# Second layer's down projection in two column halves, 19 of its 44 steps by seven block products, left-hand sums kept in memory

## The chip, the cores and the metric

The kernel runs on one core of a Trainium2 chip. The core's engines are TensorE (PE in the profile; its weight loads are PEld), VectorE (DVE), ScalarE (ACT), GpSimd (POOL) and SyncE (SP, which here only issues DMAs). The metric is device time in microseconds (us) of one execution; lower is better.

## The reference

Two decoder layers over 256 tokens, model width 2048, everything float32. Attention and the state-space mixer are not touched by this change, so only the end of a layer is shown.

```python
for l in range(DEPTH):                     # DEPTH = 2
    h = rms_norm(x, attn_norm_w[l])
    ...                                    # attention and SSD mixer, joined in mixed
    x = x + mixed
    h = rms_norm(x, ffn_norm_w[l])
    ff = (silu(h @ w_gate[l]) * (h @ w_up[l])) @ w_down[l]   # (256, 5632) @ (5632, 2048)
    x = x + ff
```

## The kernel before

**Three products for one.** Each float32 operand is split in a high part (a rounding to the type fp32r) and a low part (the rest), and each block product is three matmuls: high by high, low by high, high by low. The activations after the gate are kept so, as `f_hi` and `f_lo` (44 tiles of 128 rows by 256 tokens). Weights come from memory in pairs: a pair is 256 rows of a weight by 512 columns, 512 KB, in one of four slots of the ring `raw` (RING = 4). SyncE loads it once VectorE has split the pair four before it (`lo_split`); ScalarE writes the high part (L912; it waits until TensorE has used the pair four before, `pair_used`); VectorE subtracts to get the low part (L1169). Both do this LEAD = 3 pairs ahead of TensorE's place. So each engine walks through the same numbered pairs p = 0, 1, ..., and the rest of its work is hung on certain p in its own loop. All of it is written out by hand with semaphores; an engine does its list in order.

**The stages of a layer.** 72 pairs of the input projection, 32 of the output projection (from P_OUT), 176 of gate and up (from P_FF: 11 chunks of 512 columns, 8 pairs of gate and 8 of up each), 88 of down (from P_DOWN: four column blocks n of 512, 22 pairs each). Where the weights are the stationary operand ("turned", L744) a pair is 24 matmuls of 256 columns. In layer 1's down the activations are stationary and the weights move: a pair is 12 matmuls of 512 columns (L547; the last pair is L559, `last_products`, which does one token half after the other).

**Where the weights' high and low parts lie.** `w_hi`, `w_hi_s` and `w_hi_e` name the same ring of slots at three small offsets (0, 64 and 224 bytes on); `w_lo` likewise. Turned pairs use `_s`, and the pairs p in FURTHER_ON use `_e`. All of these are in slot 3.

**Layer 1's down in detail.** `products` adds token halves t = 0 and 1 of block n into two PSUM banks; the pairs of banks 0, 1 and 2, 3 alternate over the n. After the block, VectorE scales the two banks by the norm factor `rs` and adds them to `xr` (`add_down`, L1433). `xr` holds x turned by 128x128 tiles after the mixer, so it is turned back first: 8 transposes (`turn_back`, L581) after pair 2 of each block, and two copies on ScalarE (`back_out`, L962). SyncE stores block n while block n+1 runs, and the last block in two token halves (`store_last`, L362).

**The gate.** `form_ff` (L1451) writes silu(gate) times up for a chunk into `stage[:, 1]`; ScalarE and VectorE split it into `f_hi` (L1056) and `f_lo` (L1457).

## Time and profile before

| what | us |
|---|---|
| three timed runs: median, lowest, highest | 2111.05, 2110.71, 2111.59 |
| the profiled execution: its own time, its span | 2112.05, 2110.0 |
| TensorE, VectorE, ScalarE, GpSimd busy | 2101.6, 1269.3, 983.6, 134.3 |
| layer 1's gate and up end, down begins | 1863.5 |
| last matmul begins | 2106.3 |

The span is first to last instruction; the profiled execution's own time is 2.05 us more, and the median of the timed runs is 1.0 us under that time. A matmul's duration in the profile is from entering to leaving the array, so that matmuls overlap: their rate is read from how long a run of so many takes, not from the mean duration.

### The profile page before, as it was taken

How to read it: one execution, taken by the hardware profiler on the slowest of the kernel's cores; microseconds unless marked ns; L12 is line 12 of the kernel's file. 1: busy time of each engine (PE TensorE's matmuls, PEld its weight loads, DVE VectorE, ACT ScalarE, POOL GpSimd, SP SyncE). 2: the span in 40 equal slices, each digit the busy share in tenths (PEclk: the TensorE clock that was granted, in tenths of full speed). 3: DMA queues.
4: the chain of work that ended last, by engine and by line, in shares of the span. 5: the costliest groups of instructions: out<-in, count | busy, mean ns of one | idle time of the engine just before them, and what ended most of it. 6: DMA issues, size and time to landing. Idle time of an engine off the chain costs nothing.

```text
span 2110.0 us, 38413 instructions
## 1 busy us (share of the span) xinstructions
PE 2101.6 (100%) x16853; PEld 1998.7 (95%) x16853; DVE 1269.3 (60%) x1455; ACT 983.6 (47%) x1215; POOL 134.3 (6%) x158
## 2 busy tenths in 40 slices
PE   9999999999999999999999999999999999999999
PEld 8987899999999999999999878999999999988887
DVE  6887866555555555555578878665555555544443
ACT  5555754444444444443445556544444444443332
POOL 1034200000000000000000432000000000000000
PEclk9999999999999999999999999999999999999999
DMA  7675466666666666666666644666666666666664
GB/s 224 181 214 151 128 199 194 197 192 194 195 192 197 192 194 195 192 192 198 192 175 190 199 146 148 193 190 195 194 193 197 192 195 194 192 191 201 198 206 131
DMA packets 204518, 397.24 MB, mean 188 GB/s; under 512 B 12400, under 2 KB 12800, under 8 KB 204352
## 3 DMA queue, kind: packets, MB, share of 16 engines
q1 hardware_dynamic: 202752, 390.24, 62.6%
q0 software_dynamic: 1568, 4.56, 0.9%
q8 instruction: 132, 2.16, 0.4%
q14 instruction: 34, 0.28, 0.0%
q10 hardware_dynamic: 32, 0.01, 0.0%
HBM read 392.62 MB, written 2.13 MB: 187 GB/s over the span
## 4 chain that ended last, share of the span: by engine, by line
PE 98%; DMA 1%; ACT 1%; DVE 0%; issue 0%; SPq 0%; ACTq 0%
PE ps L744 72%; PE ps L547 22%; PE ps L581 1%; PE ps L723 1%; DMA raw<-in_w_in_dram 0%; PE ps L701 0%; PE ps L700 0%; PE ps L676 0%; DMA xr<-in_x_dram 0%; PE ps L661 0%; PE ps L623 0%; PE ps L652 0%; ACT w_hi_s L912 0%; PE ps L559 0%; SPq L326 0%
## 5 line engine op out<-in xcount | busy, mean ns | idle before, releaser
L1169 DVE TENSOR_TENSOR w_lo_s<-raw,w_hi_s 128x1024 fp32r<-128x1024 f32 x553 | 681.7, 1233 | 606.4 <-ACT w_hi_s L912 605.3
L912 ACT CAST w_hi_s<-raw 128x1024 fp32r<-128x1024 f32 x553 | 580.5, 1050 | 783.0 <-PE ps L744 767.7
L744 PE MATMUL ps<-h_hi,w_hi_s 128*128 128x256 f32 x3224 | 892.4, 277 | 1.5 <-DVE h_lo L1178 0.9
L744 PE MATMUL ps<-h_hi,w_lo_s 128*128 128x256 f32 x3224 | 890.8, 276 | 0.0
L744 PE MATMUL ps<-h_lo,w_hi_s 128*128 128x256 f32 x3224 | 890.7, 276 | 0.0
L744 PEld LDWEIGHTS ps<-h_hi,w_hi_s 128*128 128x128 f32 x3224 | 605.5, 188 | 2.1 <-DVE h_lo L1178 1.1
L744 PEld LDWEIGHTS ps<-h_lo,w_hi_s 128*128 128x128 f32 x3224 | 605.5, 188 | 0.0
L744 PEld LDWEIGHTS ps<-h_hi,w_lo_s 128*128 128x128 f32 x3224 | 605.4, 188 | 0.0
L744 PE MATMUL ps<-f_hi,w_hi_s 128*128 128x256 f32 x1192 | 330.3, 277 | 0.0
L744 PE MATMUL ps<-f_hi,w_lo_s 128*128 128x256 f32 x1192 | 329.5, 276 | 0.0
L744 PE MATMUL ps<-f_lo,w_hi_s 128*128 128x256 f32 x1192 | 329.5, 276 | 0.0
L1169 DVE TENSOR_TENSOR w_lo<-raw,w_hi 128x1024 fp32r<-128x1024 f32 x168 | 211.0, 1263 | 146.5 <-ACT w_hi L912 146.3
L912 ACT CAST w_hi<-raw 128x1024 fp32r<-128x1024 f32 x168 | 175.3, 1050 | 177.0 <-PE ps L547 166.4
L744 PEld LDWEIGHTS ps<-f_hi,w_hi_s 128*128 128x128 f32 x1192 | 223.8, 188 | 0.8 <-issue 0.7
L744 PEld LDWEIGHTS ps<-f_hi,w_lo_s 128*128 128x128 f32 x1192 | 224.0, 188 | 0.0
L744 PEld LDWEIGHTS ps<-f_lo,w_hi_s 128*128 128x128 f32 x1192 | 223.8, 188 | 0.1
L547 PE MATMUL ps<-w_hi,f_hi 128*128 128x512 f32 x348 | 107.5, 390 | 0.0
L547 PE MATMUL ps<-w_hi,f_lo 128*128 128x512 f32 x348 | 107.2, 389 | 0.0
L547 PE MATMUL ps<-w_lo,f_hi 128*128 128x512 f32 x348 | 107.1, 389 | 0.0
L547 PE MATMUL ps<-w_hi,h_hi 128*128 128x512 f32 x320 | 102.6, 402 | 0.0
L547 PE MATMUL ps<-w_hi,h_lo 128*128 128x512 f32 x320 | 98.9, 390 | 0.0
L547 PE MATMUL ps<-w_lo,h_hi 128*128 128x512 f32 x320 | 98.8, 390 | 0.0
(224 smaller groups left out, 1535.0 us busy)
## 6 DMA issues: line engine op xcount, KB each, us to landing
raw<-in_w_gate_dram SPq DMA_DIRECT2D x176, 512.0 KB, 4.4
raw<-in_w_up_dram SPq DMA_DIRECT2D x176, 512.0 KB, 4.4
raw<-in_w_down_dram SPq DMA_DIRECT2D x176, 512.0 KB, 4.2
raw<-in_w_in_dram SPq DMA_DIRECT2D x144, 512.0 KB, 3.7
raw<-in_w_out_dram SPq DMA_DIRECT2D x64, 512.0 KB, 4.2
cum_all<-cum_kept POOLq DMA_DIRECT2D x8, 512.0 KB, 4.8
xr<-in_x_dram SPq DMA_DIRECT2D x4, 512.0 KB, 9.0
out_dram<-xr SPq DMA_DIRECT2D x3, 512.0 KB, 5.9
```

Of the source, the lines that this page charges most:

```text
L547: done = nc.tensor.matmul(ps[:, bank + t, :], lhs[:, rows + k, t * P:(t + 1) * P], w[:, slot, k, :], start=(first and k == 0 and w is w_hi ...
L581: done = nc.tensor.transpose(ps[0:src.shape[1], bank + at // N, at % N:at % N + src.shape[0]], src, ident[0:src.shape[0], 0:src.shape[0]])
L723: last = nc.tensor.matmul(ps[half * HEAD:(half + 1) * HEAD, 5, keys * P:TOK], vtok[:, keys, j, :], pT[:, half, keys * TOK:TOK + keys * P], ...
L744: done = nc.tensor.matmul(ps[:, bank + m // 2, m % 2 * TOK:(m % 2 + 1) * TOK], w[:, slot, k, m * P:(m + 1) * P], h[:, rows + k, :], start= ...
L912: nc.scalar.copy(split_buffers(pair)[0][:, slot, :, :], raw[:, slot, :, :]).then_inc(hi_split, 1)
L1169: v_.tensor_tensor(lo[:, slot, :, :], raw[:, slot, :, :], hi[:, slot, :, :].bitcast(F32), ALU.subtract).then_inc(lo_split, 1)
```

## The change

**Steps instead of blocks.** Layer 1's down goes in two column halves of 1024. A step is 256 rows of `w_down` by such a half: two pairs, e = 0 and 1 (22 steps in a half, 44 in all). SyncE's load order follows. With the activations of a step as 2x2 blocks A (128 rows k by 128 tokens t) and the weights as 2x2 blocks B (k by 512 columns e), an ordinary step has eight block products, 24 matmuls (`eight_products`, L649). In steps 3, 5, ..., 19 of the first half and 1, 3, ..., 19 of the second (9 + 10 = 19) it has seven, 21 matmuls (`seven_products`, L664 to L666), by the Winograd form of Strassen's method. The four partial results of that form that more than one output shares are added up over all such steps in four PSUM banks (`sum_banks`), the other products go to the four ordinary output banks (`four_banks`); so eight banks are in use, and the two halves swap the groups. Which sums are formed:

- of the activations, four blocks of 128x128 for an odd step: GpSimd forms them as `s_raw` from `stage[:, 1]` right after `form_ff`, ScalarE and VectorE split them, GpSimd stores both parts to memory (`s_kept`, 512 KB a chunk, 10 chunks), and in the down stage loads them back into a ring of two (`load_left`, 19 loads of 512 KB);
- of the weights, four blocks of 128x512: VectorE forms them as `t_raw` (`right_sums`, one operation of 1024 columns and two of 512), ScalarE and VectorE split them (`t_hi`, `t_lo`, which lie in `h_hi` and `h_lo`; two operations of 1024 on each). Of the second pair only half has to be split itself.

**After a half** VectorE adds the shared sums: `sums_out` parts 0 to 3 (an addition and a `grow`, which scales and adds to `xr`) at its places P_DOWN + 40 to 43 of the half, then `four_out` twice (two `grow` each). ScalarE first copies one bank (`keep_first`). TensorE waits for part 3 (`sums_added`) before the second half's step 0.

**Moved.** The 32 transposes of `turn_back` now stand in layer 1's gate and up, 16 after pair P_FF + 10 and 16 after P_FF + 14; `back_out` with them, at ScalarE's places P_FF + 11 and 15. P_FF + 15 joins FURTHER_ON, in both layers. The stores of blocks 0 and 1 go out in the second half, block 2's behind the last load.

```diff
+    STEPS = {0: range(3, 20, 2), 1: range(1, 20, 2)}
+    FORMS = FCH - 1
...
+    def seven_before(half, q):
+        return half * len(STEPS[0]) + len([s for s in STEPS[half] if s < q])
...
+    def four_banks(half):
+        return [[4, 6], [5, 7]] if half == 0 else [[0, 2], [1, 3]]
+    def sum_banks(half):
+        return (0, 1, 2, 3) if half == 0 else (4, 5, 6, 7)
...
-        FURTHER_ON = (7, 15, 19, 27, P_OUT + 7, P_FF + 7, P_FF + 11, P_DOWN + 3)
+        FURTHER_ON = (7, 15, 19, 27, P_OUT + 7, P_FF + 7, P_FF + 11, P_FF + 15, P_DOWN + 3)
...
+                    if layer == DEPTH - 1:
+                        half, q, e = down_step(layer * PAIRS + p)
+                        n = 2 * half + e
...
-                    if layer == DEPTH - 1 and p >= P_DOWN + DOWN and (p - P_DOWN) % DOWN == 8:
-                        store((p - P_DOWN) // DOWN - 1)
+                    if layer == DEPTH - 1 and p in (P_DOWN + 2 * DOWN + 10, P_DOWN + 2 * DOWN + 14):
+                        store((p - P_DOWN - 2 * DOWN - 10) // 4)
+            store(2)
...
+                v = stage[:, 1, 1, :]
+                a11, a21, a12, a22 = (v[:, i * P:(i + 1) * P] for i in range(4))
+                own.done(pool.tensor_tensor(s_raw[:, 0, :], a21, a22, ALU.add))
+                own.done(pool.tensor_tensor(s_raw[:, 1, :], s_raw[:, 0, :], a11, ALU.subtract))
+                pool.tensor_tensor(s_raw[:, 2, :], a11, a21, ALU.subtract)
+                pool.tensor_tensor(s_raw[:, 3, :], a12, s_raw[:, 1, :], ALU.subtract).then_inc(s_formed, 1)
...
+                pool.dma_start(s_kept[c, :, 0, :, :], s_hi).then_inc(s_stored, 16)
+                pool.dma_start(s_kept[c, :, 1, :, :], s_raw.bitcast(F32R)).then_inc(s_stored, 16)
...
+                i = seven_before(half, q)
+                if i >= 2:
+                    pool.wait_ge(s_used, i - 1)
+                pool.dma_start(s_ring[:, i % 2], s_kept[q // 2]).then_inc(s_landed[i % 2], 16)
...
+            def seven_products(pair, half, q):
...
+                i, slot = seven_before(half, q), pair % RING
+                first, last = q == STEPS[half][0], q == STEPS[half][-1]
+                (b11, b12), (b21, _) = four_banks(half)
+                b1, b5, b7, b6 = sum_banks(half)
+                s = s_ring[:, i % 2]
+                def product(bank, left_hi, left_lo, right_hi, right_lo, opens=False, closes=False):
+                    nc.tensor.matmul(ps[:, bank, :], left_hi, right_hi, start=opens, stop=False)
+                    nc.tensor.matmul(ps[:, bank, :], left_lo, right_hi, start=False, stop=False)
+                    return nc.tensor.matmul(ps[:, bank, :], left_hi, right_lo, start=False, stop=closes)
...
+                pe.wait_ge(lo_split, pair + (1 + RING))
+                product(b1, *left(0, 0), w_hi[:, slot, 0, :], w_lo[:, slot, 0, :], first, last)
+                product(b11, *left(1, 0), w_hi[:, slot, 1, :], w_lo[:, slot, 1, :]).then_inc(pair_used, 1)
+                pe.wait_ge(lo_split, pair + (2 + RING))
+                pe.wait_ge(s_landed[i % 2], 16 * (i // 2 + 1))
+                product(b12, *mixed(3), w_hi[:, slot + 1, 1, :], w_lo[:, slot + 1, 1, :]).then_inc(pair_used, 1)
+                pe.wait_ge(t_split, 2 * i + 1)
+                product(b5, *mixed(0), *summed(0, 0), first, last)
+                product(b7, *mixed(2), *summed(0, 1), first, last).then_inc(t_used, 1)
+                pe.wait_ge(t_split, 2 * i + 2)
+                product(b6, *mixed(1), *summed(1, 0), first, last).then_inc(s_used, 1)
+                product(b21, *left(1, 1), *summed(1, 1)).then_inc(t_used, 1)
...
+                        if layer == DEPTH - 1 and c == 0 and q in (2, 6):
+                            if q == 2:
+                                pe.wait_ge(rsb_ready, layer * 2 + 2)
+                            else:
+                                pe.wait_ge(back_ready, 2)
+                            for n in range(q // 2 - 1, q // 2 + 1):
+                                turn_back(n)
...
+                            if half and q == 0:
+                                pe.wait_ge(sums_added, 1)
+                            if half and q == STEPS[1][0]:
+                                pe.wait_ge(down_added, layer * DCH + 2)
+                            if seven(pair):
+                                seven_products(pair, half, q)
+                            else:
+                                eight_products(pair, half, q, 0)
...
-                nc.scalar.copy(split_buffers(pair)[0][:, slot, :, :], raw[:, slot, :, :]).then_inc(hi_split, 1)
+                if not seven(pair) or down_step(pair)[2] == 0:
+                    nc.scalar.copy(split_buffers(pair)[0][:, slot, :, :], raw[:, slot, :, :]).then_inc(hi_split, 1)
+                    return
+                nc.scalar.copy(w_hi[:, slot, 1, :], raw[:, slot, 1, :]).then_inc(hi_split, 1)
+                i = seven_before(*down_step(pair)[:2])
+                for a in range(2):
+                    act.wait_ge(t_formed, 2 * i + a + 1)
+                    if i:
+                        act.wait_ge(t_used, 2 * i + a - 1)
+                    nc.scalar.copy(t_hi[:, a], t_raw[:, a]).then_inc(t_hi_ready, 1)
...
+            def keep_first(half):
+                act.wait_ge(t_used, 2 * seven_before(half, DOWN))
+                nc.scalar.copy(stage[:, 0, 0, :], ps[:, sum_banks(half)[0], :]).then_inc(first_kept, 1)
...
+                v_.tensor_tensor(lo[:, slot, 1, :], raw[:, slot, 1, :], hi[:, slot, 1, :].bitcast(F32),
...
+                for a in range(2):
+                    dve.wait_ge(t_hi_ready, 2 * i + a + 1)
+                    v_.tensor_tensor(t_lo[:, a], t_raw[:, a], t_hi[:, a].bitcast(F32), ALU.subtract).then_inc(t_split, 1)
...
+            def right_sums(pair):
+                slot, i = pair % RING, seven_before(*down_step(pair)[:2])
+                if i == 0:
+                    dve.wait_ge(pair_used, (DEPTH - 1) * PAIRS + P_DOWN + RING)
+                else:
+                    dve.wait_ge(t_split, 2 * i)
+                for j in range(2):
+                    dve.wait_ge(raw_landed[slot + j], 16 * (pair // RING + 1))
+                v_.tensor_tensor(t_raw[:, 0], raw[:, slot + 1, :, :], raw[:, slot:slot + 2, 0, :], ALU.subtract) \
+                    .then_inc(t_formed, 1)
+                dve.wait_ge(t_formed, 2 * i + 1)
+                own.done(v_.tensor_tensor(t_raw[:, 1, 0, :], raw[:, slot + 1, 1, :], t_raw[:, 0, 0, :], ALU.subtract))
+                v_.tensor_tensor(t_raw[:, 1, 1, :], raw[:, slot, 1, :], t_raw[:, 1, 0, :], ALU.subtract) \
+                    .then_inc(t_formed, 1)
...
+                u1, u2, u4, u5 = stage[:, 0, 0, :], stage[:, 0, 1, :], stage[:, 1, 0, :], stage[:, 1, 1, :]
+                if part == 0:
+                    dve.wait_ge(first_kept, half + 1)
+                    own.done(v_.tensor_tensor(u2, b6, u1, ALU.add))
+                    grow(rows(0, 0), 0, b1)
+                if part == 1:
+                    own.done(v_.tensor_tensor(u4, b5, u2, ALU.add))
+                    grow(rows(0, 1), 0, u4)
+                if part == 2:
+                    own.done(v_.tensor_tensor(u5, b7, u4, ALU.add))
+                    grow(rows(1, 1), 1, u5)
+                if part == 3:
+                    own.done(v_.tensor_tensor(u2, b7, u2, ALU.add))
+                    grow(rows(1, 0), 1, u2).then_inc(sums_added, 1)
+                    dve.wait_ge(sums_added, half + 1)
...
+            def four_out(half, e):
...
+                    last = v_.scalar_tensor_tensor(v, ps[:, four_banks(half)[t][e], :], rs[:, t:t + 1], v,
+                                                   ALU.mult, ALU.add)
...
-                    if base + p + LEAD < ALL:
-                        split_lo(base + p + LEAD)
+                    ahead_pair = base + p + LEAD
+                    if ahead_pair < ALL:
+                        if seven(ahead_pair) and down_step(ahead_pair)[2] == 0:
+                            right_sums(ahead_pair)
+                        split_lo(ahead_pair)
...
+                        half, q, e = down_step(base + p)
+                        if q >= DOWN - 2:
+                            sums_out(half, 2 * (q - DOWN + 2) + e)
+                        if q == DOWN - 1 and e:
+                            four_out(half, 0)
+                            four_out(half, 1)
```

TensorE in layer 1's down, before, around the transposes of a block (`f_hi`, `f_lo` are the activations):

```order
L547 MATMUL ps<-w_hi,f_hi 128x512 x2
L547 MATMUL ps<-w_hi,f_lo 128x512 x2
L547 MATMUL ps<-w_lo,f_hi 128x512 x2
L581 MATMUL ps<-ident,xr 128x128 x8
L547 MATMUL ps<-w_hi,f_hi 128x512 x2
```

and now, in a step of seven, three of its block products (`h_lo` is here the ring of loaded sums as left operand and `t_lo` as right one, `h_hi` is `t_hi`):

```order
L664 MATMUL ps<-w_hi,f_hi 128x512
L665 MATMUL ps<-w_hi,f_lo 128x512
L666 MATMUL ps<-w_lo,f_hi 128x512
L664 MATMUL ps<-w_hi,h_lo 128x512
L665 MATMUL ps<-w_hi,h_lo 128x512
L666 MATMUL ps<-w_lo,h_lo 128x512
L664 MATMUL ps<-h_hi,h_lo 128x512
L665 MATMUL ps<-h_hi,h_lo 128x512
L666 MATMUL ps<-h_lo 128x512
```

The pairs' x2 (both token halves by one weight block) became triples that each go to one bank, and the transposes have left the stage.

TensorE in layer 1's first chunk of the up projection, before, where pair P_FF + 10 ends and the pair P_FF + 11, in `_e`, begins:

```order
L744 MATMUL ps<-h_hi,w_hi_s 128x256
L744 MATMUL ps<-h_lo,w_hi_s 128x256
L744 MATMUL ps<-h_hi,w_lo_s 128x256
L744 MATMUL ps<-h_hi,w_hi_e 128x256
L744 MATMUL ps<-h_lo,w_hi_e 128x256
```

and now:

```order
L871 MATMUL ps<-h_hi,w_hi_s 128x256
L871 MATMUL ps<-h_lo,w_hi_s 128x256
L871 MATMUL ps<-h_hi,w_lo_s 128x256
L708 MATMUL ps<-ident,xr 128x128 x16
L871 MATMUL ps<-h_hi,w_hi_e 128x256
L871 MATMUL ps<-h_lo,w_hi_e 128x256
L871 MATMUL ps<-h_hi,w_lo_e 128x256
```

Sixteen transposes came between the two; the same stands after P_FF + 14, whose next pair is now in `_e` too.

VectorE in layer 1's down, before, from the first block's end on (`add_down` is L1433):

```order
L1169 TENSOR_TENSOR w_lo<-raw,w_hi 128x1024 x20
L1433 SCALAR_TENSOR_TENSOR xr<-ps,rs,xr 128x512 x2
L1169 TENSOR_TENSOR w_lo<-raw,w_hi 128x1024 x22
L1433 SCALAR_TENSOR_TENSOR xr<-ps,rs,xr 128x512 x2
L1169 TENSOR_TENSOR w_lo<-raw,w_hi 128x1024 x22
```

and now, at the end of the first half, from part 1 of `sums_out` on (L1391, L1394, L1397 are additions of parts 1, 2, 3; L1383 is `grow`; L1363 to L1367 are `right_sums`; L1414 is `four_out`):

```order
L1391 TENSOR_TENSOR stage<-ps,stage 128x512
L1383 SCALAR_TENSOR_TENSOR xr<-stage,rs,xr 128x512
L1344 TENSOR_TENSOR w_lo<-raw,w_hi 128x1024
L1394 TENSOR_TENSOR stage<-ps,stage 128x512
L1383 SCALAR_TENSOR_TENSOR xr<-stage,rs,xr 128x512
L1363 TENSOR_TENSOR t_raw<-raw 128x1024
L1366 TENSOR_TENSOR t_raw<-raw,t_raw 128x512
L1367 TENSOR_TENSOR t_raw<-raw,t_raw 128x512
L1344 TENSOR_TENSOR w_lo<-raw,w_hi 128x1024
L1397 TENSOR_TENSOR stage<-ps,stage 128x512
L1383 SCALAR_TENSOR_TENSOR xr<-stage,rs,xr 128x512
L1414 SCALAR_TENSOR_TENSOR xr<-ps,rs,xr 128x512 x4
```

The right-hand sums of the second half's step 1 and the split of its first pair stand ahead of part 3, for which TensorE waits.

## Rows read from the trace of the kernel before

**Rows 1.** The page, chain that ended last: shares of the span by engine.
```profile
PE 98%; DMA 1%; ACT 1%; DVE 0%; issue 0%; SPq 0%; ACTq 0%
```

**Rows 2.** Chain that ended last, 1800 to 2110: start us, us, what.
```profile
1799.89 63.81 PE ps L744 x563
...
1871.89 0.88 PE ps L581 x8
1872.77 59.85 PE ps L547 x264
...
2103.97 2.73 PE ps L559 x12
...
2106.73 0.75 DVE xr L1433
```

**Rows 3.** Busy by window: PE, PEld, DVE, ACT, POOL; clock, DMA share, GB/s.
```profile
1950.00:2000.00 50.00, 50.00 (x226) 41.46 (x225) 23.38 (x20) 19.97 (x21) 0.00 (x0) 1.00 0.66 196
```

**Rows 4.** Groups, 1880 to 2110: busy us, mean ns of one, idle before.
```profile
L1169 DVE TENSOR_TENSOR w_lo<-raw,w_hi 128x1024 fp32r<-128x1024 f32 x80 | 98.0, 1225 | 117.2 <-ACT w_hi L912 117.2
L912 ACT CAST w_hi<-raw 128x1024 fp32r<-128x1024 f32 x79 | 82.9, 1049 | 124.3 <-PE ps L547 124.3
...
L1433 DVE SCALAR_TENSOR_TENSOR xr<-ps,rs,xr 128x512 f32<-128x512 f32 x8 | 5.7, 748 | 8.9 <-PE ps L559 7.8 <-PE ps L547 1.1
L962 ACT COPY xr<-ps 128x512 f32<-128x512 f32 x6 | 3.2, 590 | 7.5 <-PE ps L581 7.5
```

**Rows 5.** Timeline of VectorE, 1863 to 1867.5: start, duration, instruction.
```profile
1863.74 1.23 DVE L1451 TENSOR_TENSOR stage<-ps,stage 128x1024 f32<-128x1024 f32 x1 [0.36 <-PE ps L744]
1864.88 1.23 DVE L1169 TENSOR_TENSOR w_lo<-raw,w_hi 128x1024 fp32r<-128x1024 f32 x1
```

**Rows 6.** Timeline, all engines, 1990 to 2012: a pair's start and its split.
```profile
2005.00 0.62 PE L547 MATMUL ps<-w_hi,f_hi 128*128 128x512 f32 x2
...
2005.25 1.05 ACT L912 CAST w_hi<-raw 128x1024 fp32r<-128x1024 f32 x1 [1.67 <-PE ps L547]
...
2006.33 1.23 DVE L1169 TENSOR_TENSOR w_lo<-raw,w_hi 128x1024 fp32r<-128x1024 f32 x1 [1.50 <-ACT w_hi L912]
```

**Rows 7.** Landing of `w_down` loads, all 176.
```profile
DMA to landing us min/median/max: 3.5/4.2/5.9
```

**Rows 8.** `cum_all`'s loads by GpSimd: issue ns, and landing.
```profile
L480 POOL DMA_DIRECT2D cum_all<-cum_kept x8: 530/590/635, 112.5 to 1191.0; - x8
...
DMA to landing us min/median/max: 4.1/4.8/6.1
```

**Rows 9.** DMA rate in 40 slices of 2080 to 2110; landing of its stores.
```profile
GB/s 96 229 320 87 117 322 219 71 145 358 145 112 248 303 46 0 0 0 0 0 0 0 0 0 0 0 0 0 0 0 0 0 0 0 0 0 344 63 292 0
...
out_dram<-xr SPq DMA_DIRECT2D x2, 256.0 KB, 2.1
```

**Rows 10.** The page's DMA issues: the stores of 512 KB.
```profile
out_dram<-xr SPq DMA_DIRECT2D x3, 512.0 KB, 5.9
```

**Rows 11.** Chain, 1250 to 1500, layer 1's P_FF + 4 and on.
```profile
1397.50 0.34 PE ps L605 x4
1397.84 11.30 PE ps L744 x96
...
1409.35 90.66 PE ps L744 x799
```

**Rows 12.** Chain, 1060 to 1120, layer 1's first pairs.
```profile
1075.70 8.47 PE ps L744 x72
...
1086.40 11.31 PE ps L744 x96
```

**Rows 13.** Tile `w_hi_e`, 1070 to 1090: where its matmuls stand.
```profile
L744 PE MATMUL ps<-h_hi,w_hi_e x8: 277/279/281, 1078.5 to 1080.9; 128*128 128x256 f32 x8
```

**Rows 14.** Waits of TensorE over the span: total us, times, longest.
```profile
PE ps L744 <- DVE h_lo L1178: 0.9, 1, 0.9
```

**Rows 15.** Tile `dist` on GpSimd: an addition of 128x128.
```profile
L422 POOL TENSOR_TENSOR dist<-dist,ahead x1: 454/454/454, 4.2 to 4.2; 128x128 f32<-128x128 f32 x1
```

More of the change, by code:

```diff
@@ L92, in weights_stationary, with down_step, seven @@
         return p < 4 * PPG or P_OUT <= p < P_DOWN or p >= P_DOWN and layer < DEPTH - 1
+    def down_step(pair):
+        layer, p = pair // PAIRS, pair % PAIRS
+        if layer < DEPTH - 1 or p < P_DOWN:
+            return None
+        half, rest = divmod(p - P_DOWN, 2 * DOWN)
+        return half, rest // 2, rest % 2
+    def seven(pair):
+        step = down_step(pair)
+        return step is not None and step[1] in STEPS[step[0]]
+    def seven_before(half, q):
[4 more added lines that the diff above has]
+        return (0, 1, 2, 3) if half == 0 else (4, 5, 6, 7)
     def bank_of(layer, idx):
@@ L154, in split_buffers @@
             return (w_hi_e, w_lo_e) if pair % PAIRS in FURTHER_ON else (w_hi_s, w_lo_s)
+        at_h = 83456
         xr = sb("xr", [P, T, D], F32, 128)
@@ L551, in products, with last_products @@
                 done.then_inc(pair_used, 1)
-            def last_products(slot, pair, rows, bank):
+            def last_products(slot, pair, rows, banks):
                 pe.wait_ge(lo_split, pair + (1 + RING))
@@ L558, in last_products, with eight_products @@
                         for lhs, w in ((f_hi, w_hi), (f_lo, w_hi), (f_hi, w_lo)):
-                            done = nc.tensor.matmul(ps[:, bank + t, :], lhs[:, rows + k, t * P:(t + 1) * P],
+                            done = nc.tensor.matmul(ps[:, banks[t], :], lhs[:, rows + k, t * P:(t + 1) * P],
                                                     w[:, slot, k, :], start=False, stop=(k == 1 and w is w_lo))
                     done.then_inc((half_done, pair_used)[t], 1)
+            def eight_products(pair, half, q, e):
+                slot, last = pair % RING, q == DOWN - 1
+                pe.wait_ge(lo_split, pair + (1 + RING))
+                for k in range(2):
+                    for lhs, w in ((f_hi, w_hi), (f_lo, w_hi), (f_hi, w_lo)):
+                        for t in range(T):
+                            done = nc.tensor.matmul(ps[:, four_banks(half)[t][e], :],
+                                                    lhs[:, 2 * q + k, t * P:(t + 1) * P], w[:, slot, k, :],
+                                                    start=(q == 0 and k == 0 and w is w_hi and lhs is f_hi),
+                                                    stop=(last and k == 1 and w is w_lo))
+                done.then_inc(pair_used, 1)
@@ new lines, in left_lo, with sums_out, rows, grow @@
+            def left_lo(c):
+                dve.wait_ge(s_hi_ready, c + 1)
+                v_.tensor_tensor(s_raw.bitcast(F32R), s_raw, s_hi.bitcast(F32), ALU.subtract).then_inc(s_split, 1)
+            def sums_out(half, part):
+                b1, b5, b7, b6 = (ps[:, b, :] for b in sum_banks(half))
+                def rows(t, e):
+                    n = 2 * half + e
+                    return xr[:, t, n * N:(n + 1) * N]
+                def grow(v, t, by):
+                    return v_.scalar_tensor_tensor(v, by, rs[:, t:t + 1], v, ALU.mult, ALU.add)
+                u1, u2, u4, u5 = stage[:, 0, 0, :], stage[:, 0, 1, :], stage[:, 1, 0, :], stage[:, 1, 1, :]
[13 more added lines that the diff above has]
+                    dve.wait_ge(sums_added, half + 1)
@@ new lines, in four_out @@
+            def four_out(half, e):
+                n = 2 * half + e
+                final = n == DCH - 1
+                if not final:
+                    dve.wait_ge(pair_used, (DEPTH - 1) * PAIRS + P_DOWN + 2 * (half + 1) * DOWN - 1 + e + RING)
+                for t in range(T):
+                    v = xr[:, t, n * N:(n + 1) * N]
+                    if final and t == 0:
+                        dve.wait_ge(half_done, 1)
+                    elif final:
+                        last.then_inc(down_added, 1)
+                        dve.wait_ge(pair_used, ALL + RING)
+                    last = v_.scalar_tensor_tensor(v, ps[:, four_banks(half)[t][e], :], rs[:, t:t + 1], v,
+                                                   ALU.mult, ALU.add)
+                last.then_inc(down_added, 1)
```

112 lines of the change are left out of this document (78 added, 34 removed).

## Prediction, made before the run

> **What bounds the kernel.** I read first the chain that ended last. It is TensorE for 98% of the span, with nothing in it that another engine holds up [rows 1]: so a matmul taken away is worth its whole interval, and a matmul that has to wait costs the whole wait. Then the rates. In layer 1's down 264 matmuls of 512 columns take 59.85 us, 226.7 ns each; the last twelve, which go six in a row to one bank, take 2.73 us, 227.5 ns each, so neither the order of the banks nor the wait at each pair shows [rows 2]. A pair of 12 is 2.72 us. In the turned stage before it 563 matmuls of 256 columns take 63.81 us, 113.3 ns each [rows 2]. Last, what stands beside: in 50 us of down VectorE is busy 23.4 and ScalarE 20.0, the granted clock is 1.00 (the 2.4 GHz level) and the DMA engines are busy 0.66 of the time at 196 GB/s [rows 3].
>
> **What goes.** A step of seven has 21 matmuls for 24. 19 steps x 3 x 226.7 ns = 12.92 us [rows 2]. The operands keep their size, and each is 512-byte aligned as before, so I take the same rate for the triples into one bank, on the evidence of the last twelve; the far end is a rate of 227.5 for all 399 matmuls of these steps, 0.3 us, and below nothing I see no reason for a gain.
>
> **What moves.** Four groups of eight transposes, 0.88 us each [rows 2], leave down and cost the same in gate and up: nought. Their copies are 8 x 0.59 us on ScalarE [rows 4]. They go in two lots of 2.4 us, while a pair is split once in 2.72 us with 1.05 of work and three pairs of lead: covered.
>
> **Does the feed keep up?** From the issue of one step of seven to the next, with one of eight between, TensorE now has 45 matmuls, 10.20 us. Let the first begin at 0: its first pair is used at 1.36, its second at 2.04, `t_hi`'s first half at 3.40, all at 4.76; the step of eight uses its pairs at 7.48 and 10.20. Latencies: ScalarE starts 0.25 us after a pair's end and takes 1.05, VectorE follows 0.03 later [rows 6]. VectorE's 1024 columns last 1.23 us, but the next operation starts after 1.14 [rows 5]; 512 columns no row shows behind another: half of 1.14 is 0.57, and 0.75 is one alone out of PSUM [rows 4]. I take 0.6 in the steps and 0.75 for the sums after a half, which read PSUM. Where one waits for the one before I add 0.1. VectorE: split of the last pair before, done at 2.5; right-hand sums of the next step, 1.14 + 0.7 + 0.7, done at 5.05 (with 0.75 for 0.6, three times a round, 0.45 more of its 10.20); split of its first pair 6.2, half of its second 6.8, `t_lo` 7.95 and 9.1; the next pair's split 10.25; then it idles 1.3 us until ScalarE has the high part of the pair that comes free at 10.20, at 11.5, and is done at 12.7, that is 2.5 of the next round. The circle closes: VectorE has 8.9 us of work in 10.20. TensorE wants the first pair at 10.20 (it was there at 6.2), `t_lo` at 12.24 and 13.6 (there at 7.95 and 9.1): at least 4.0 us of slack. So nothing is lost in the steps themselves. If that cover went, a round would last as long as VectorE's work.
>
> **Loads.** The sums need `w_down`'s second pair, whose load is issued when the half split of the second pair before is done, at -3.4, and is wanted at 2.5: 5.9 us. Loads land in 3.5 to 5.9, median 4.2 [rows 7]; beside GpSimd's loads of the same size those take 4.1 to 6.1 [rows 8]. Traffic rises to five loads of 512 KB in 10.20 us, 257 GB/s, DMA busy 0.66 x 257/196 = 0.87; single slices reach 358 GB/s [rows 9]. Here three loads are issued within 2 us (-5.2, -4.0, -3.4), 1.5 MB, 4.4 us at that rate, so I expect 5 to 5.5 for the last. A landing 0.3 late a round would eat 5 us of idle time and slack over a half: hardly visible. Cost taken: 0, ends 0 and 3.
>
> **The middle (a new wait).** Before, one block's sums were added while the next block used two other banks. Now all eight are in use, and the second half's step 0 needs the banks of the shared sums. Let T be the end of the last step of seven of the first half; four pairs follow, so TensorE is ready at T + 10.88. VectorE has split pair 43 of the stage at T + 0.25. `keep_first` runs T + 0.25 to 0.85. Part 0 (two of 0.75 at most [rows 4]) ends at 2.4. Pair 44 is free to be overwritten at 2.72, its high part there at 4.0, low part at 5.2; part 1 ends at 6.7. Pair 45: 6.75 and 7.95; part 2 ends at 9.4. Now, ahead of part 3, come the right-hand sums of pair 46 (2.55) and its split (1.15): 13.1. Part 3 ends at 14.65. TensorE starts at about 14.85: **it waits 4.0 us**. Queued behind the waiting matmul is all of TensorE's work; behind VectorE's part 3 are four `grow` and the split of pair 47, which end at 17.8 and 18.4 and are wanted by step 1 at 20.3 and 21.7: no second wait. Ends: 2.5, if the operations of 512 columns overlap as those of 1024 do, and 5.5, if each of the eight dependences costs 0.3 more than I gave it.
>
> The chip may take that wait amiss. The granted clock is 1.00 in every window, and after the start TensorE never idles longer than 0.9 us [rows 14], so no row tells what 4 us of idleness do. If TensorE came back at the 1.2 GHz level, half the clock could at worst double the 226.7 ns of the next step's 24 matmuls: +5.4 us. I take 0 and keep the other end for the range. On this the Trainium skill ("TensorE: Matmul & The Clock Gate", section "Part 1: The HAM clock gate") says that an idle TensorE drops to 1.2 GHz, the low level, and has to be busy for a while to get the high one back: a rule that speaks against the change, and no run here yet shows it.
>
> **The end.** `sums_out` of the second half lies under the last four pairs (no split stands between, part 3 ends at T' + 6.5), and the last `grow` of 0.75 after the last matmul is as before [rows 2]. But block 2's store of 512 KB, before under the last block, is now issued about 1.8 us before the last 256 KB: 1 MB in 2 us. The last landed in 2.1; 512 KB ones took 5.9 under load [rows 9, 10]. At 344 GB/s [rows 9] 1 MB takes 3.0 us, so the last lands 0.6 later; ends 0 and 2.
>
> **Gate and up, layer 1.** GpSimd's four additions are about 0.45 each [rows 15], over a whole chunk of 43 us; ScalarE's and VectorE's extra 512 columns fit in their idle time; a store of 512 KB a chunk adds 12 GB/s. Nought. The further `_e` pair in each layer costs at most the slow rate of rival A, 0.106 us: 0.2.
>
> **Sum**: -12.9 + 4.0 + 0.6 + 0.2 + 0 = -8.1 us. The profiled execution took 2112.05, so 2103.9; the median of the runs is 1.0 less, **2103**.
>
> **Rivals.**
>
> *A, slower: the turned stage stays at its slow rate.* The stage has two rates. After a foreign matmul at P_FF + 4 the next 96 go at 11.30 us, 117.7 ns, and with the pair after the `_e` pair the rate is back at 113.4 [rows 11]. In layer 1's first pairs an `_e` pair [rows 13] did not do it: 72 matmuls with it in their middle took 117.6 ns each and the 96 behind 117.8 [rows 12]. The change puts 32 transposes in front of the FF's fast stretch, with an `_e` pair directly behind each lot, a placing that no row shows. If the slow rate survives P_FF + 15, 160 pairs follow at 24 x 4.4 ns = 0.106 us more: +16.9, 2120. It decides from 77 slow pairs on (8.1 / 0.106). For it: one failure in the trace; against: the later `_e` pairs all restored the rate, and slow stretches there were short.
>
> *B: loads or VectorE bind.* If the last load of a bunch takes L, a round is at least 4.3 + L. At L = 6.3 that is 10.6; 17 rounds lose 6.8 less the slack of 4 in each half, mostly hidden, but the middle's wait grows by what VectorE is behind, up to 4: 2107. At L = 7, 11.3 a round, 19 less 8 of slack: 2114; from L = 7.1 it is slower by what can be told. For it: 0.87 of the DMA time and bunches; against: 6.1 is the longest seen beside GpSimd's loads. The Trainium skill ("Trainium Kernel Development and Optimization", section "Key Constraints") states that DMAs issued by SP and by GpSimd share the same 16 engines and interleave, which agrees with the longer landings [rows 8] and speaks for B: a second queue would bring no second path.
>
> *C: the middle costs nothing*, or little, since VectorE is faster than I count: 2099 to 2100.
>
> *D: the clock falls after the wait*, for all or part of the next step: 2105 to 2108. For and against: above, at the middle.
>
> *E: the products don't run at 226.7*, since three left operands come from freshly loaded memory and the right one from another place; at 236 ns (4% more) the 399 matmuls give 3.7 us back: 2106.7. Nothing in the trace speaks for it.
>
> **Numbers.** Forecast 0.62 (2101 to 2105.5), A 0.10, B 0.10 (a third of it slower or no gain), C 0.07, D 0.07, E 0.04. What a measurement of this kernel can tell from no change is about 0.2%, 4.2 us: faster is under 2106.8, slower over 2115.3. Faster: forecast, C, most of D, half of E and of B: 0.80; same 0.09 (the rest of B, D and E); slower 0.11 (A and the worst of B). The range leaves out A and the worst of B: 2099 to 2110.
>
> **What would show it.** Right: down lasts 243.2 - 3.5 - 12.9 + 4.0 = 231 us; triples at 226.7 ns; one wait of TensorE of about 4 us on VectorE between the halves, and no other over 0.3; VectorE busy near 88% in down; gate and up at 113.3 from P_FF + 16 on. Wrong: many small waits of TensorE on `t_lo` (B), 117.7 ns through gate and up (A), a granted clock under 1.00 after the middle (D). A time over 2110 would refute the sum, one under 2099 the wait in the middle.

## The result, and the profile after

| kernel | median us (lowest to highest) | ratio to before, 95% interval |
|---|---|---|
| before | 2110.88 (2110.52 to 2111.59) | 1 |
| changed | 2121.57 (2121.04 to 2122.30) | 1.0050 (1.0033 to 1.0068) |

The change made the kernel slower by 10.7 us; 2103 was forecast, 2110 was the upper end. Of all executions used below one, of 7500 us, of `after_sums_first_b`, was disturbed: it is among the five of that median and not in the ratio beside it. The profiled execution of the changed kernel took 2121.89 us, its span is 2120.2, 10.2 more than before. That splits by stage:

| stretch | before | changed | difference |
|---|---|---|---|
| start to the matmuls of `x_total` in layer 1 (after P_FF + 4) | 1397.50 | 1396.76 | -0.7 |
| from there to the first matmul of layer 1's down | 466.0 | 487.0 | +21.0 |
| down, first to last matmul | 242.8 | 232.6 | -10.1 |
| last matmul to the end | 3.7 | 3.75 | +0.05 |

So down gained nearly what was promised, and gate and up lost twice that. The chain that ended last, changed kernel, 1380 to 2125 (start, us, what), to be held against [rows 11]:

```profile
1396.76 0.34 PE ps L732 x4
1397.10 11.30 PE ps L871 x96
...
1414.09 1.75 PE ps L708 x16
1415.83 11.29 PE ps L871 x96
1427.12 1.75 PE ps L708 x16
1428.87 455.08 PE ps L871 x3864
```

After the first lot of transposes 96 matmuls take 11.29 us, 117.6 ns each, and after the second lot all 3864 of the rest take 117.8 ns. Before, the same stretch ran at 113.3: in 350 us of gate and up 3091 matmuls began before and 2974 now. The two rows, before and changed, in that order (columns as in [rows 3]):

```profile
1500.00:1850.00 350.00, 350.00 (x3091) 350.00 (x3090) 185.38 (x153) 151.75 (x145) 0.00 (x0) 1.00 0.67 194
```

```profile
1500.00:1850.00 350.00, 350.00 (x2974) 350.00 (x2974) 183.97 (x156) 150.72 (x148) 29.42 (x46) 1.00 0.67 197
```

TensorE's row reads "busy 350.00 of 350.00" in both, and the granted clock is 1.00 in both. Only the count tells that the engine is 4% slower. Down itself, from the same chain: an ordinary step is 5.44 us as before, and the steps of seven follow at the same interval.

```profile
1905.05 5.44 PE ps L649 x24
1910.72 0.23 PE ps L665
1910.95 0.23 PE ps L666
...
1915.25 5.44 PE ps L649 x24
...
2001.04 8.32 PE ps L649 x24
...
2114.09 2.73 PE ps L638 x12
2116.84 0.75 DVE xr L1414
```

From 1905.05 to 1915.25 is 10.20 us for the 45 matmuls of two steps, 226.7 ns each. One ordinary step, at 2001.04, took 8.32: it is the first of the second half, right behind the wait in the middle. TensorE's waits (total, times, longest), then the windows around it:

```profile
PE ps L649 <- DVE xr L1383: 3.5, 1, 3.5
PE ps L895 <- POOL numbers L455: 2.2, 1, 2.2
```

```profile
1996.00:2001.00 5.00, 1.53 (x7) 0.94 (x5) 4.89 (x6) 2.51 (x3) 0.00 (x0) 0.87 0.35 99
2001.00:2006.00 5.00, 4.96 (x12) 3.89 (x13) 4.97 (x7) 0.00 (x0) 0.00 (x0) 0.50 0.42 120
2006.00:2011.00 5.00, 5.00 (x22) 4.09 (x21) 2.30 (x3) 2.28 (x3) 0.00 (x0) 0.95 0.43 127
```

The granted clock, 1.00 until then, is 0.50 (the 1.2 GHz level) for the 5 us behind the wait, and the matmuls that begin there are 427 ns apart. The next matmul had been due at 1997.37, so the wait cost 3.67 us; the 3.5 of the list is counted from the modelled end of the last one. What VectorE did in the wait (its timeline, 1993 to 2001.5):

```profile
1995.13 0.75 DVE L1383 SCALAR_TENSOR_TENSOR xr<-stage,rs,xr 128x512 f32<-128x512 f32 x1
1995.80 1.22 DVE L1363 TENSOR_TENSOR t_raw<-raw 128x1024 f32<-128x1024 f32 x1
1997.05 0.69 DVE L1366 TENSOR_TENSOR t_raw<-raw,t_raw 128x512 f32<-128x512 f32 x1
1997.78 0.69 DVE L1367 TENSOR_TENSOR t_raw<-raw,t_raw 128x512 f32<-128x512 f32 x1
1998.39 1.22 DVE L1344 TENSOR_TENSOR w_lo<-raw,w_hi 128x1024 fp32r<-128x1024 f32 x1
1999.52 0.68 DVE L1397 TENSOR_TENSOR stage<-ps,stage 128x512 f32<-128x512 f32 x1
2000.24 0.75 DVE L1383 SCALAR_TENSOR_TENSOR xr<-stage,rs,xr 128x512 f32<-128x512 f32 x1
```

The right-hand sums (2.6 us) and a split (1.1 us) stand between part 2 and part 3, as the order of the program has it. Part 3 ends at 2000.99, and TensorE goes on at 2001.04.

The landing of all 176 loads of `w_down`, for [rows 7], and who waited for them (us, times):

```profile
  ACT w_hi L1064: 20.7, 17
  DVE t_raw L1363: 15.5, 15
...
DMA to landing us min/median/max: 3.5/4.4/7.1
```

A load takes up to 7.1 us, VectorE waits for loads 15 times ahead of the right-hand sums, and yet TensorE's list of waits in down has no load and no `w_lo`: the slack covers it. The last three stores (512, 256, 256 KB) land in 2.7, 2.8 and 2.1 us, so the tail is as long as before.

Down accounts for itself: -12.9 (57 matmuls), -3.9 (the transposes left: 3.5, and 0.35 at the four returns from them), +3.7 (the wait), +2.9 (8.32 - 5.44, the low clock) gives -10.2, and -10.1 was measured. What had to be found out is the +21.0: 3.5 are the transposes that moved in, and the 96 and 3864 matmuls behind them, 466.4 us in the chain above, would have taken 448.7 at 113.3 ns: 17.7. Together that is 21.2; the 0.2 too much is rounding and the pair P_FF + 11 in `_e`, which took 2.80 us for 2.72 in the kernel before too.

### The profile page after: what moved, and what is told of

Same layout as the page of the kernel before. It is cut to its first block, busy times and chain, and to the rows that moved or that the text cites. A ratio compares the mean times of both kernels' runs of the same rounds, so it can differ in the third digit from the quotient of the medians.

```text
span 2120.2 us, 38631 instructions
## 1 busy us (share of the span) xinstructions
PE 2107.9 (99%) x16796; PEld 2006.3 (95%) x16796; DVE 1362.8 (64%) x1576; ACT 1020.0 (48%) x1265; POOL 183.3 (9%) x237
## 4 chain that ended last, share of the span: by engine, by line
PE 98%; ACT 1%; DVE 1%; issue 0%; DMA 0%; ACTq 0%
PE ps L871 73%; PE ps L626 10%; PE ps L649 6%; PE ps L666 1%; PE ps L665 1%; PE ps L664 1%; PE ps L708 1%; PE ps L850 1%; PE ps L828 0%; PE ps L827 0%; PE ps L803 0%; DMA xr<-in_x_dram 0%; ACT stage L1112 0%; PE ps L788 0%; DMA raw<-in_w_in_dram 0%
## 5 line engine op out<-in xcount | busy, mean ns | idle before, releaser
L1064 ACT CAST w_hi<-raw 128x1024 fp32r<-128x1024 f32 x149 | 155.4, 1051 | 119.2 <-PE ps L649 47.5
L1344 DVE TENSOR_TENSOR w_lo<-raw,w_hi 128x1024 fp32r<-128x1024 f32 x149 | 186.6, 1264 | 37.5 <-ACT w_hi L1064 36.9
L626 PEld LDWEIGHTS ps<-w_hi,h_hi 128*128 128x128 f32 x320 | 58.4, 188 | 16.1 <-issue 5.3
L626 PEld LDWEIGHTS ps<-w_hi,h_lo 128*128 128x128 f32 x320 | 60.1, 188 | 12.8
```

The costliest lines, as they stand in the source:

```text
L626: done = nc.tensor.matmul(ps[:, bank + t, :], lhs[:, rows + k, t * P:(t + 1) * P], w[:, slot, k, :], start=(first and k == 0 and w is w_hi ...
L1064: nc.scalar.copy(split_buffers(pair)[0][:, slot, :, :], raw[:, slot, :, :]).then_inc(hi_split, 1)
L1344: v_.tensor_tensor(lo[:, slot, :, :], raw[:, slot, :, :], hi[:, slot, :, :].bitcast(F32), ALU.subtract).then_inc(lo_split, 1)
```

## Experiments

Each time beside a ratio is the median of its runs, with the runs of the kernel before on the same chip.

**1. Which part makes gate and up slow?** The change brings three things there: transposes, GpSimd's sums with their stores, and a further `_e` pair. `before_moved_b` is the kernel before with the transposes and their copies moved and with the further `_e` pair, without the sums:

```diff
-        FURTHER_ON = (..., P_FF + 7, P_FF + 11, P_DOWN + 3)
+        FURTHER_ON = (..., P_FF + 7, P_FF + 11, P_FF + 15, P_DOWN + 3)
...
+                        if layer == DEPTH - 1 and c == 0 and q in (2, 6):
...
+                            for n in range(q // 2 - 1, q // 2 + 1):
+                                turn_back(n)
...
-                        if layer == DEPTH - 1 and q == 2:
-                            turn_back(n)
```

> The kernel before with one part of the change alone: the 32 transposes and their copies stand in layer 1's gate and up (16 after pair P_FF + 10, 16 after P_FF + 14) and P_FF + 15 is an _e pair; down is in blocks of eight products as before. Theory 1 (the transposes put the turned stage at its slow rate and the _e pair directly behind does not end it) and theory 2 (so many transposes leave a slow state that no _e pair ends) both say: 160 pairs at 117.8 instead of 113.3 ns, 24 x 4.5 ns x 160 = 17.3 us, so about 2128. Theory 3 (the slow rate comes from the other parts of the change, GpSimd's sums and stores or the longer program): about 2111, gate and up at 113.3.

Measured: 2128.99, ratio 1.0082 (1.0067 to 1.0097), 18 us over before, with nothing of Strassen in it. Its chain and its window of 350 us:

```profile
1416.04 11.29 PE ps L744 x96
1427.33 1.75 PE ps L581 x16
1429.08 71.00 PE ps L744 x603
```

```profile
1500.00:1850.00 350.00, 350.00 (x2974) 350.00 (x2973) 179.17 (x148) 146.68 (x140) 0.00 (x0) 1.00 0.65 187
```

The same 2974 matmuls, with GpSimd idle (0.00) and no more GB/s than before. So it is not the sums, their stores or their memory. That it is not the `_e` pair either, part 4 shows, which takes it out. The copies of `back_out` (2.4 us of ScalarE a lot) always came with the transposes, and no run tells the two apart, though the matmuls stay slow for 455 us after the last copy.

**2. Can an `_e` pair farther behind give the rate back?** `after_e19_b` is the changed kernel with the `_e` pair four pairs later:

```diff
-        FURTHER_ON = (..., P_FF + 11, P_FF + 15, P_DOWN + 3)
+        FURTHER_ON = (..., P_FF + 11, P_FF + 19, P_DOWN + 3)
```

> The changed kernel with P_FF + 19 in FURTHER_ON in place of P_FF + 15: the last lot of transposes (after P_FF + 14) is followed by four ordinary pairs, the last three before the _e pair being those of slots 0, 1, 2. Theory 1: 113.3 ns from P_FF + 20 on, 156 pairs x 0.108 = 16.8 us less than the changed kernel, about 2104.7. Theories 2 and 3: still slow, 2121.6.

Measured: 2104.94, ratio 0.9968 (0.9955 to 0.9981).

```profile
1427.76 1.75 PE ps L708 x16
1429.51 70.57 PE ps L871 x618
```

```profile
1500.00:1850.00 350.00, 350.00 (x3090) 350.00 (x3089) 190.91 (x161) 156.93 (x154) 30.62 (x48) 1.00 0.71 206
```

The matmuls are slow up to P_FF + 19, and fast from P_FF + 20 to the end of the stage. One number in the code is worth 16.6 us. So the loss is the rate of the matmuls and nothing else: the work is the same, transposes included, at the same places.

`after_slot0_b` puts each lot of transposes ahead of two ordinary pairs and these ahead of an `_e` pair:

```diff
-                        if layer == DEPTH - 1 and c == 0 and q in (2, 6):
+                        if layer == DEPTH - 1 and c == 0 and q == 4:
...
+                        if layer == DEPTH - 1 and c == 1 and q == 0:
...
+        FURTHER_ON = (..., P_FF + 11, P_FF + 15, P_FF + 19, P_DOWN + 3)
```

> The changed kernel with the two lots of transposes after pairs P_FF + 12 and P_FF + 16 (slot 0) and _e pairs at P_FF + 15 and P_FF + 19, so two ordinary pairs and then the _e pair follow each lot, as in the places of the kernel before where the rate came back. Theory 1: 113.3 ns from P_FF + 20 on, about 2104.6. Theories 2 and 3: 2121.6.

Measured: 2104.25, ratio 0.9967 (0.9955 to 0.9980). In its chain the 96 matmuls after a lot take 11.20 us, two slow pairs, the `_e` pair and a fast one; then 576 take 65.57, 113.8 each.

**3. How many ordinary pairs does it take?** `after_slot1`: the second lot one pair later, so that one ordinary pair stands between it and the `_e` pair.

```diff
-                        if layer == DEPTH - 1 and c == 1 and q == 0:
+                        if layer == DEPTH - 1 and c == 1 and q == 1:
```

> The changed kernel with the first lot of transposes after P_FF + 12 (slot 0) and the second after P_FF + 17 (slot 1), _e pairs at P_FF + 15 and P_FF + 19: one ordinary pair stands between the second lot and its _e pair. If an _e pair ends the slow rate only with two or more ordinary pairs ahead of it (as all places show where it did), gate and up stay at 117.8 ns from P_FF + 18 on: 156 pairs x 0.108 = 16.8 us over the 2104.25 of the kernel with two, about 2121. If one pair is enough: 2104.

Measured: 2105.18 in one run, which with its window of 3091 matmuls is enough to tell it from 2121. One ordinary pair is enough here. Yet in [rows 12] of the kernel before one ordinary pair stood there too, and the rate did not come back. What tells these two apart stays open.

**4. Is it the `_e` pair at all?** Three kernels without it. `after_no_e15` is the changed kernel, `slot0_v2_no_e` is `slot0_v2` (below), `before_no_e` the kernel before:

```diff
-        FURTHER_ON = (..., P_FF + 7, P_FF + 11, P_FF + 15, P_DOWN + 3)
+        FURTHER_ON = (..., P_FF + 7, P_FF + 11, P_DOWN + 3)
```

```diff
-        FURTHER_ON = (..., P_FF + 7, P_FF + 11, P_FF + 15, P_FF + 19, P_DOWN + 3)
+        FURTHER_ON = (..., P_FF + 7, P_FF + 11, P_DOWN + 3)
```

```diff
-        FURTHER_ON = (..., P_OUT + 7, P_FF + 7, P_FF + 11, P_DOWN + 3)
+        FURTHER_ON = (..., P_OUT + 7, P_DOWN + 3)
```

> The changed kernel without its new _e pair P_FF + 15. If an _e pair directly behind transposes does nothing: gate and up slow as they are, 2121.6. If it is this pair that keeps the rate slow: 113.3 ns from P_FF + 16 or soon after, about 2104.5.

> The 2099.69 us kernel (transposes after P_FF + 12 and P_FF + 16, 18 steps of seven, part 3 first) without the _e pairs P_FF + 15 and P_FF + 19. If after these transposes only an _e pair with an ordinary pair ahead of it restores the rate: slow from P_FF + 13 to the end, 163 pairs x 0.108 = 17.6 us against the 4 to 5 slow pairs now, about 2116.7. If transposes between slots 0 and 1 are harmless by themselves, as the two after P_FF + 8 were: 2099.5.

> The kernel before without the _e pairs P_FF + 7 and P_FF + 11, in both layers. If an _e pair is what brings the rate back after the foreign matmuls at P_FF + 4 and + 8: 117.8 ns for all of gate and up from there, 167 to 171 pairs x 0.108 in each layer, 36 to 37 us more, 2147 to 2148. If the rate comes back by itself, or with the two transposes after P_FF + 8: 2111. If in one layer only: about 2129.

Measured: `after_no_e15` 2119.30, ratio 1.0042 (1.0026 to 1.0058), still 2974 matmuls in the window: directly behind the transposes the `_e` pair does nothing (the 2.3 us under the changed kernel are the clock, part 7). `slot0_v2_no_e` 2116.38, 1.0024 (1.0014 to 1.0034), against 2099.69 with it: 16.7 us, so behind 16 transposes it is the `_e` pair that gives the rate back. `before_no_e` 2111.45, 1.0000 (0.9989 to 1.0010), where I had expected 2147. Its chain:

```profile
1397.12 11.41 PE ps L744 x96
1408.54 0.22 PE ps L753 x2
1408.75 91.26 PE ps L744 x805
```

The 805 matmuls take 113.4 ns each with no `_e` pair near: here the two transposes of L753 (`spread_rs`) stand where the rate comes back, after one more slow pair. Did the `_e` pair P_FF + 7 then do nothing in [rows 11]? The 96 matmuls ahead of L753 take 11.30 us there and 11.41 here, and the difference lies in pair P_FF + 8, the one behind the `_e` pair (first matmul of the pair and what follows it; before, then `before_no_e`):

```profile
1406.23 0.28 PE L744 MATMUL ps<-h_hi,w_hi_s 128*128 128x256 f32 x1
...
1408.97 0.38 PE L753 MATMUL ps<-ident,rs 128*128 128x128 f32 x2
```

```profile
1405.55 0.28 PE L744 MATMUL ps<-h_hi,w_hi_s 128*128 128x256 f32 x1
...
1408.37 0.38 PE L753 MATMUL ps<-ident,rs 128*128 128x128 f32 x2
```

The pair takes 2.74 us behind the `_e` pair and 2.82 without it. So the `_e` pair did bring the rate back, by this one pair. Then come the two transposes, and in both kernels P_FF + 9 is slow (2.83) and P_FF + 10 fast (2.72): P_FF + 11 had nothing left to restore. What I had read out of [rows 11] as the work of the `_e` pairs was for the most part that of the two transposes.

The traces tell early which way it goes, by the first pair behind foreign matmuls. In layer 1 of the kernel before it takes 2.82 to 2.84 us where the rate comes back by itself (two transposes at 1097.55, eight at 1108.75), and 2.91 where the stage stays slow behind it (eight transposes at 1309.12, up to the next `_e` pair); behind the lots of 16 it takes 2.89 to 2.92. So neither the number of transposes alone nor their kind decides it. At 52 us, where `before` and `before_no_e` are still the same program, that pair took 2.91 in one and 2.82 in the other, so the instructions alone don't decide it either. Whether fewer than 16 transposes at the new places would have kept the rate was not tried.

**5. The wait in the middle.** `after_sums_first_b` puts part 3 ahead of the right-hand sums of pair 46:

```diff
+                    if layer == DEPTH - 1 and p >= P_DOWN and down_step(base + p)[1:] == (DOWN - 1, 1):
+                        sums_out(down_step(base + p)[0], 3)
                     ahead_pair = base + p + LEAD
...
-                        if q >= DOWN - 2:
+                        if q >= DOWN - 2 and (q, e) != (DOWN - 1, 1):
```

> The changed kernel, but VectorE does part 3 of the shared sums before the right-hand sums and the split of pair 46, not behind them. If the wait in the middle (3.5 us) is made by that order, it shrinks to 0.2 or less, and if the clock's fall to 0.50 (24 matmuls in 8.32 us for 5.44, +2.9) comes from that wait, it goes too: 6.2 us less, of which a new wait of up to 1.1 us before the second half's step 1 (VectorE's four grow now come 1.1 us later than that step can start) gives some back: 2115.5 to 2116.5. If the clock falls for another reason: about 2118.5 to 2119.5. Gate and up stay slow.

Measured: 2118.72, ratio 1.0035 (1.0020 to 1.0049); 2.9 us under the changed kernel, not the 5 to 6 expected. TensorE's waits and the chain that ended last, 1990 to 2060:

```profile
PE ps L664 <- DVE w_lo L1344: 1.4, 2, 1.1
PE ps L664 <- DVE xr L1414: 0.7, 1, 0.7
```

```profile
2013.13 1.38 SPq L398
2014.55 6.37 DMA raw<-in_w_down_dram
2021.04 1.24 DVE t_raw L1363
...
2025.29 0.47 SPq L398
2025.81 6.67 DMA raw<-in_w_down_dram
2032.60 1.24 DVE t_raw L1363
...
2036.47 0.50 PE ps L664
```

The clock stays at 1.00 and the long wait is gone, but the work that was pushed back, and two loads of 6.4 and 6.7 us with the block stores of L398 issued between them, now reach TensorE in three small waits, ahead of three of the first four steps of seven of the second half: 2.1 us by the list, 2.9 in the gaps between the matmuls. Down lasts 229.4 us, 3.2 less than in the changed kernel. The first of the three is the four `grow` of VectorE (L1414); the two others lead back to the loads. That is rival B, hidden in the changed kernel by the wait in the middle.

**6. The version that follows.** `slot0_v2`: the places of `after_slot0_b`, part 3 first, and one step of seven less at the start of the second half, where the loads were late:

```diff
-    STEPS = {0: range(3, 20, 2), 1: range(1, 20, 2)}
+    STEPS = {0: range(3, 20, 2), 1: range(3, 20, 2)}
```

> The kernel with the transposes after slot 0 (2104.25), and in the middle both: part 3 of the shared sums ahead of VectorE's work for later pairs, and the second half's first step of seven at step 3 in place of 1 (18 steps of seven), so that no right-hand sums are due between the halves. Theory: the wait in the middle was only VectorE's order; it goes from 3.67 us to 0.3 or less, and the clock's fall behind it (1.2 us in that kernel's profile) goes too; the lost step of seven costs 0.68: 4.2 us less, about 2100. With sums ahead and step 1 still of seven, TensorE waited 2.5 us in three places of the second half instead, since VectorE started it late; here VectorE has two steps' time to catch up, so none of these. Rival (VectorE or the loads bind in the second half as soon as TensorE no longer waits in the middle): waits of 1 to 2 us on the weights' low parts, 2101 to 2102.

Measured: **2099.69** (2099.39 to 2100.10), ratio 0.9944 (0.9929 to 0.9959), the fastest of all. Down lasts 227.0 us from the first matmul to the last, and 88 pairs of 2.72 less 18 x 3 matmuls of 0.2267 are 227.1. TensorE waits for nothing in down.

`slot0_few` takes the steps of seven down to one a half (`range(19, 20, 2)`) and leaves all else:

> The same kernel with one step of seven in each half (step 19) in place of nine: 16 steps go back to eight products, 48 matmuls of 226.7 ns, 10.9 us more than with 18 steps, about 2111. If the extra loads, sums and splits of the steps of seven cost TensorE anything beside its own matmuls, the difference is less than 10.9.

Measured: 2110.68, ratio 0.9996 (0.9986 to 1.0006), 11.0 us over `slot0_v2`; 16 steps x 3 x 0.2267 are 10.9. The windows of down, `slot0_v2` and `slot0_few`:

```profile
1870.00:2090.00 220.00, 220.00 (x972) 182.08 (x971) 190.10 (x195) 118.62 (x122) 8.44 (x16) 1.00 0.75 242
```

```profile
1870.00:2100.00 230.00, 230.00 (x1016) 190.26 (x1015) 124.85 (x114) 92.03 (x90) 0.00 (x0) 1.00 0.64 195
```

VectorE's share goes from 0.54 to 0.86 and the bytes from 195 to 242 GB/s, and TensorE loses nothing by it: 972 matmuls in 220 us are 226.3 ns each, 1016 in 230 are 226.4. So in this kernel Strassen's steps are worth just what they leave out.

`slot0_v2_late` is `slot0_v2` with part 3 in its old place:

```diff
-                    if layer == DEPTH - 1 and p >= P_DOWN and down_step(base + p)[1:] == (DOWN - 1, 1):
-                        sums_out(down_step(base + p)[0], 3)
...
-                        if q >= DOWN - 2 and (q, e) != (DOWN - 1, 1):
+                        if q >= DOWN - 2:
```

> The 2099.69 us kernel with part 3 back in its old place, behind the split of pair 46; no right-hand sums stand there any more. TensorE then waits in the middle for that split alone, 1.15 us and the hand-over, 1.2 to 1.4 us, in place of 3.67. If the clock falls only after a longer idle stretch: granted clock 1.0 throughout and 2101.0. If any wait of over a microsecond here brings it down: 1.1 to 2.9 us more, 2102 to 2104.

Measured: 2100.59, ratio 0.9949 (0.9933 to 0.9966). TensorE stands 1.3 us (1.1 in its list of waits) in place of 3.7, at full clock in all four executions: without right-hand sums for step 1 (2.6 us) part 3 comes 2.4 us sooner, which confirms what stood in its way.

**7. The clock.** `after_no_e15` has the wait of the changed kernel, 3.5 us in both lists. Its windows of 5 us from 1995:

```profile
1995.00:2000.00 5.00, 2.50 (x12) 1.73 (x10) 4.90 (x7) 3.33 (x4) 0.00 (x0) 1.00 0.36 115
2000.00:2005.00 5.00, 3.98 (x17) 3.30 (x18) 4.93 (x8) 0.97 (x2) 0.00 (x0) 1.00 0.38 107
```

Here the clock stays at 1.00, and down lasts 230.1 for 232.6 us. Its three executions took 2119.0, 2119.3 and 2122.1: the last is 2.8 longer, and it alone shows a mean clock under 1.000 (0.998). So with the same 3.7 us of idleness the fall comes in some executions and not in others. By the mean clock it came in all four of the changed kernel, all six of `after_slot0_b`, four of five of `after_e19_b`, the one of `after_slot1`, and one of three here. What it costs is read from the first step of the second half, 5.44 us at full clock with nothing ahead of it: 5.74 here, without a fall, 7.24 in `after_slot0_b` (1.8 over; the 1.2 in the expectation of `slot0_v2` is too low), 7.35 in `after_e19_b` (1.9), 8.32 in the changed kernel (2.9), 8.59 in `after_slot1` (3.2).

## Why the prediction was wrong

- **Gate and up, layer 1: "Nought". This is the step that failed.** It allowed 0.2 us for the `_e` pairs and 0 for the transposes ("cost the same in gate and up"), and 17.7 us came. I priced the work that moved and not what it does to the rate of the 3960 matmuls behind it. *Shown*: by `before_moved_b`, which loses 18 us without the sums, by `after_no_e15`, which is as slow without the `_e` pair, and by `after_e19_b` with the rate restored.
- **Rival A was what happened**, and its price held: 16.9 us and 2120 were forecast, 17.7 and 2121.6 measured (the fall of the clock, rival D, came on top). Its chance of 0.10 was far too low. It rested on "the later `_e` pairs all restored the rate". Some did: P_FF + 7 for one pair, and by the look of it the one behind eight transposes at 1309.12. But the rate is back for good at P_FF + 10 with or without the `_e` pairs (`before_no_e`), and several `_e` pairs, P_FF + 11 among them, stood in a stage that was fast already. So this counted for much less than it seemed, while the one plain failure of an `_e` pair [rows 12] was waved off as one against several, and none of those that worked stood directly behind the foreign matmuls. The chain rows before and after a place show a change of rate; they do not show its cause.
- **What goes**: right. 226.7 ns in the steps of seven, 11.0 for 10.9 us in `slot0_few` against `slot0_v2`. Rival E is out.
- **The feed**: right in the result. No wait of TensorE in the steps of the changed kernel, VectorE busy 85% of down (88 forecast). The size of the landings was off: up to 7.1 for the 5 to 5.5 expected of the last of three. That rival B did not bind was in part luck, the middle's doing: with its wait gone, 2.9 us of gaps came out (`after_sums_first_b`).
- **The middle**: mechanism and size right (4.0 forecast, 3.7 measured), and the right-hand sums ahead of part 3 are its cause. Rival C is out.
- **The clock, rival D**: 0 was taken, 2.9 came in the profiled execution, with 5.4 as the far end. In its direction this agrees with what the prediction quotes from the Trainium skill ("TensorE: Matmul & The Clock Gate", section "Part 1: The HAM clock gate"), that an idle TensorE drops to the 1.2 GHz level. That a fall does not always follow, the runs add: two of the three executions of `after_no_e15` show none.
- **The tail**: 0.6 forecast, 0.05 measured; the 256 KB landed in 2.1 as before.

By its own terms, with the rate kept, the forecast would have been good: `after_e19_b`, the same work with the `_e` pair elsewhere, took 2104.9, where 2103 was predicted and the fall of the clock, 1.9 us there, not counted.

What stays open is what the two rates are. The runs show when the matmuls go over to 117.8 ns and what brings them back, not the state in the engine or its memory that stands behind it.

## What to carry to other kernels

A stage whose matmuls issue back to back can have two sustained rates, as this one has, that the busy time doesn't show: count matmuls in equal windows, before and after, ahead of all other reading. When foreign matmuls are put into such a stage, price every matmul that follows them, not only the ones put in; and when a restoring trick stands in the trace, prove by taking it out that it is the trick that restores. A wait taken away on the engine that bounds may only uncover the next one, so take the slack of the feed with it.

## What the runs showed of the hardware

- 128x256 matmuls with their weight loads ran at 113.3 or at 117.8 ns each, for over 400 us on end, at a granted clock of 1.00 and a busy time of 100% in both. Each lot of 16 transposes (with its copies on ScalarE) brought the slow rate; two or eight transposes brought it in some places and cost one slow pair in others. A pair of weights at another offset in memory, with four, two or one ordinary pairs ahead of it, brought the fast one (2104.9, 2104.3, 2105.2), though once, with one pair ahead, it did not [rows 12]; directly behind the transposes it did nothing (2121.6, 2129.0), and without it the slow rate lasted to the end of the stage (2116.4 for 2099.7). At full clock matmuls of 512 columns ran at 226.7 ns after slow stages and fast ones.
- After an idle stretch of 3.7 us the granted clock fell in 16 of 19 executions of five kernels, to 0.50 in the changed kernel's profile; with `after_no_e15` it fell in one of three. The fall cost 1.8 to 3.2 us. After 1.3 us (`slot0_v2_late`) it fell in none of four.
- With loads of 512 KB issued in bunches, and GpSimd's beside them, they landed in up to 7.1 us, at a DMA share of 0.74 in the mean; in the kernel before, which spaces them, 5.9 was the longest. No run parts the bunching from the higher traffic.
